# GpSimd adds the squares of six RMS norms; TensorE multiplies the mean matrix with one or two tiles a norm, behind the second weight slot

## The chip, the cores and the metric

One core of one Trainium2 chip runs the whole program. The metric is the device time of one execution in microseconds (us), the median of a few runs. Lower is better.

## What is computed

One inference step of a decoder trunk of two layers for 264 tokens (256 of a prompt and 8 samples of one token), in float32, with a model width of 1024:

```python
def rmsnorm(x, w):
    xf = x.astype(jnp.float32)
    y = xf * lax.rsqrt(jnp.mean(xf * xf, axis=-1, keepdims=True) + EPS)
    return (y * w.astype(jnp.float32)).astype(x.dtype)

def swiglu(h, wg, wu, wd):
    return (jax.nn.silu(h @ wg) * (h @ wu)) @ wd

for li in range(2):
    x = x + 0.5 * swiglu(rmsnorm(x, norm_ffn1[li]), ...)        # 1024 -> 2816 -> 1024
    h = rmsnorm(x, norm_mix[li])
    y = even_mixer(h, ...) if li == 0 else pool_mixer(h, ...)   # HGRN2 || gated DeltaNet; pooling
    x = x + y
    x = x + 0.5 * swiglu(rmsnorm(x, norm_ffn2[li]), ...)
y = rmsnorm(x, final_norm)
```

That makes seven RMS norms, numbered 0 to 6 in the kernel. The recurrent states are outputs too; the change does not touch them.

## The kernel before

**Layout.** Everything is held transposed: `x` has 8 tiles of 128 channels (partitions) by 264 tokens. The mean of squares over the 1024 channels is then a sum over partitions and tiles. TensorE makes it: ScalarE squares each tile of `x` into `hn`, and TensorE multiplies a 128x128 matrix `mean_w`, filled with 1/1024, with the eight tiles of `hn`, all summed in one PSUM bank (`sum_bank(n)`: bank 0, for norm 5 bank 2). Every row of that bank then holds the mean for each token.

**Weights.** All big matmuls use weights in pieces of 128x1024 floats, the slots, counted through the program by `s`. SyncE loads a slot into `raw` (4 buffers). ScalarE rounds it to `w_hi` (the ScalarE `tick`, L504 to L512) and VectorE makes `w_lo = raw - w_hi` (the VectorE `tick`, L1007 to L1014), each 3 slots ahead of TensorE. Activations are split in the same way, and `three` (L1500) makes each product from three matmuls. A slot is 24 of them in the stages that read `xw` or `x`, and 24 in the down projection. The semaphore `used` tells ScalarE that a slot is free, `lo_done` tells TensorE that one is ready.

**The norm is deferred.** The first product behind a norm does not wait for it: it takes `xw_hi`/`xw_lo`, the split of x times the norm's weight, and the factor `rstd` is multiplied in when the result leaves PSUM. `rstd` is made by a square root on ScalarE (`root`, L532, which waits for `ss_done` from TensorE) and a reciprocal on VectorE (`root_inverse`, L1042).

**An FFN** (`ffn`, TensorE L1544 to L1601) has 11 blocks of four slots: two slots give the gate in two PSUM banks, two give the up product in the next two. Then 22 slots of the down projection fill all eight banks. VectorE multiplies the gate by `rstd` (`gate`, L1065), ScalarE makes the SiLU (`silu`, L548), VectorE makes `factor` and `prod`. TensorE starts a block only when the SiLU of the block before is done (`silu_done`, L1552).

**The end of an FFN and the norm behind it** are the place of the change. For each of the eight tiles, in this order: VectorE adds the result to `x` (`residual`, L1021), ScalarE squares the tile (`square`, L514, semaphore `sq_done`) and writes `xw_hi` (L529), VectorE writes `xw_lo` (`weighted`, L1034). TensorE in its own order, with `norm` at L1526 and `first_slot` at L1539: the last down projections; four mean matmuls (tiles 0 to 3); the first weight slot of the next stage, which waits tile by tile for `xw_lo`; four more mean matmuls (tiles 4 to 7, the last raises `ss_done`); the second slot, and on. Norm 2 follows the even mixer's output projection, norm 5 the pooling mixer, and norm 6, the last, stands among the transposes that bring the result back (L1634 to L1649).

**After a norm, by stage.** The even mixer (norm 1) reads `xw` in its first four slots only, waits for the root behind two of them (L1180), and takes the really normed `hn`, split into `x_hi` and `x_lo` by `normed` (L536 and L1047), for the other 28. The pooling mixer (norm 4) keeps VectorE busy with window sums; ScalarE's `norm(5)` stands behind its copy of the last pooled rows (L489). The order on each engine is the order of the code. GpSimd (L1652 on) makes constants at the start and then only issues DMAs.

Of the kernel before, what the change touches and what calls it, by code (L numbers as in the profile page):

```python
# [29 lines left out]
ALU = mybir.AluOpType  # L30
# [25 lines left out]
SSB = 0  # L56
# [15 lines left out]
def build(nc, A, O_):  # L72
# [9 lines left out]
    with ctx:  # L82
# [68 lines left out]
        def SV(j):  # L151
# [4 lines left out]
            if j in (4, 5):  # L156
# [38 lines left out]
         par_in, x_in, x_T, dve_chain, act_chain, pool_chain) = [sem(n) for n in (  # L195
# [3 lines left out]
             "x_in", "x_T", "dve_chain",  # L199
# [21 lines left out]

        def sum_bank(n):

            return 2 if n == 5 else SSB

# [269 lines left out]
        def _(act):  # L495
# [502 lines left out]
        def _(dve):  # L998
# [22 lines left out]
            def residual(scale, ended, n=None, tiles=range(KD)):  # L1021

                for z in tiles:
                    d = ORDER5[z] if n == 5 else z
# [9 lines left out]
            def weighted(n, z):  # L1034

                dve.wait_ge(xwhi_done, 8 * n + z + 1)
                d = ORDER5[z] if n == 5 else z
# [24 lines left out]
            def ffn(n):  # L1062
                s0, b0 = S_FFN[n], NB * n

                def gate(b, i=None):  # L1065
# [4 lines left out]
                    st4 = 4 * ((b - b0 + 1) % 2)  # L1070
# [8 lines left out]
                def prod(b, i=None):  # L1079
                    dve.wait_ge(sg_done, v(b + 1, i, 2))  # L1080
                    dve.wait_ge(used, v(s0 + 4 * (b - b0) + 4, i, 8))
                    st4 = 4 * ((b - b0 + 1) % 2) + 2
# [41 lines left out]
                residual(0.5, lambda d: (res_done, 8 * n + d + 1), FFN_NORM[n] + 1)  # L1124
# [50 lines left out]
        def even_tensor(pe, mm, three, blk_slot, first_slot, xw_slot, norm):  # L1175
            tr = nc.tensor.transpose
            nwait = (lambda k: (xlo_done, k + 1))
            first_slot(S_PROJ, 2, 1)
            xw_slot(S_PROJ + 1, 1, 2, 1)
# [273 lines left out]
            norm(2)  # L1453

        def odd_tensor(pe, mm, three, first_slot, xw_slot, norm):
# [4 lines left out]
            first_slot(S_PIN, 2, 4)  # L1460
# [7 lines left out]
            for q in range(1, 8):  # L1468
                banks = (2 * (q // 2) + 2) % 8
                if banks == SSB and q % 2 == 0:  # L1470
# [4 lines left out]
                xw_slot(S_PIN + q, q % 2, banks, 4 if q == 1 else None)  # L1475
# [17 lines left out]
            norm(5)  # L1493
# [3 lines left out]
        def _(pe):  # L1497
# [28 lines left out]
            def norm(n, tiles=range(4), frees_slot=False):  # L1526

                for z in tiles:  # L1530
                    d = ORDER5[z] if n == 5 else z
                    pe.wait_ge(sq_done, 8 * n + z + 1)
                    ins = mm(ps[:, sum_bank(n), 0:TOK], mean_w[:, :], hn[:, d, :], start=z == 0, stop=z == KD - 1)  # L1533
                    if z == 0 and frees_slot:
                        ins.then_inc(used, 1)
                    if z == KD - 1:
                        ins.then_inc(ss_done, 1)

            def first_slot(s, banks, n):  # L1539
                pe.wait_ge(x_done, 8 * n + (4 if n == 5 else banks + 2))  # L1540
                xw_slot(s, 0, banks, n)
                norm(n, range(4, KD))

            def ffn(n):  # L1544
                s0, b0, nn = S_FFN[n], NB * n, FFN_NORM[n]

                def blk(b, i=None):
                    s = s0 + 4 * (b - b0)
                    banks = 4 * ((b - b0 + 1) % 2)
                    for q in range(4):  # L1550
                        if b and q == 0:
                            pe.wait_ge(silu_done, v(b, i, 2))  # L1552
                        if b and q == 2:
                            pe.wait_ge(prod_done, v(b, i, 2))
                        if b == b0 and q == 0:
                            first_slot(s, banks, nn)
                        else:
                            if b == b0 and q == 2:
                                pe.wait_ge(x_done, 8 * nn + 8)
                            xw_slot(s + q, q % 2, banks + 2 * (q // 2),  # L1560
                                    nn if b == b0 and (q == 1 or nn == 5) else None, i)
# [19 lines left out]
                down(0, range(4))  # L1581
                down(1, range(4))
                pe.wait_ge(prod_done, b0 + NB)
                down(0, range(4, 8)).then_inc(used, 1)
                down(1, range(4, 8)).then_inc(used, 1)
# [10 lines left out]
                for d in range(KD):  # L1596
# [3 lines left out]
                    down(KF - 1, [d]).then_inc(res_done, 1)  # L1600
                norm(nn + 1, frees_slot=True)  # L1601
# [189 lines left out]
```

## Time and profile before

| what | us |
|---|---|
| median of 3 runs | 1108.94 |
| lowest and highest | 1107.06, 1110.87 |
| span of the profiled execution, first to last instruction | 1105.1 |
| TensorE matmuls busy | 1077.1 (97%) |
| VectorE busy | 670.5 (61%) |
| ScalarE busy | 520.6 (47%) |
| GpSimd busy | 47.7 (4%) |
| mean granted TensorE clock, share of full speed | 0.993 |

The profile gives for the profiled execution its span alone; its device time with what lies before the first and after the last instruction is not told apart from the runs. The span is 2.0 us under the fastest run and 3.8 us under the median. Times in the rows are in us from the start of the span, durations of single instructions in ns where it says so. PE is TensorE, DVE is VectorE, ACT is ScalarE, POOL is GpSimd. `L1533` is a line of the kernel.

### The profile page before, as it was taken

Reading aid. Unit: us, or ns where it says so; the run is one execution under the profiler, and the core shown is the slowest. Engines: PE = TensorE matmul, PEld = TensorE weight load, DVE = VectorE, ACT = ScalarE, POOL = GpSimd, SP = SyncE. Lnnn points to the kernel's source line nnn. Section 1 sums busy time; section 2 is a strip of 40 time slices with the busy share of each in tenths; the row PEclk is TensorE's granted clock in tenths of the full one; section 3 lists DMA queues with packets and bytes.
Section 4 is the critical chain, followed back from the end, with each engine's and each line's share of the span. In section 5 each row is a group of like instructions: output and inputs, shape, how many; then the busy total and the mean of one; then the engine's idle time right before and its main releaser. Section 6 shows DMA issues by size and latency. Waiting matters only on the chain.

```text
span 1105.1 us, 21620 instructions
## 1 busy us (share of the span) xinstructions
PE 1077.1 (97%) x8541; PEld 1053.1 (95%) x8541; DVE 670.5 (61%) x872; ACT 520.6 (47%) x703; POOL 47.7 (4%) x118
## 2 busy tenths in 40 slices
PE   6999999999899998999999999999999999999998
PEld 5999999989799996999999999999999989999997
DVE  5766654587555655766665457666644876666542
ACT  5444443566574443554444346444433554444434
POOL 8100000010000110000000000000000000000000
PEclk9999999999899999999999999999999999999999
DMA  6666555878485521676565555665555446665551
GB/s 195 192 176 184 174 185 174 153 202 150 109 108 137 144 77 39 188 195 186 173 186 173 181 164 172 175 186 173 171 189 183 123 117 182 180 173 188 175 169 40
DMA packets 135061, 177.91 MB, mean 161 GB/s; under 512 B 5806, under 2 KB 120574, under 8 KB 134992
## 3 DMA queue, kind: packets, MB, share of 16 engines
q1 hardware_dynamic: 131616, 165.78, 52.9%
q0 software_dynamic: 3328, 11.38, 3.6%
q8 instruction: 37, 0.61, 0.2%
q14 instruction: 16, 0.13, 0.0%
q10 hardware_dynamic: 64, 0.02, 0.0%
HBM read 171.19 MB, written 6.52 MB: 161 GB/s over the span
## 4 chain that ended last, share of the span: by engine, by line
PE 91%; DVE 4%; ACT 2%; DMA 2%; issue 1%; ACTq 0%; SPq 0%; DVEq 0%
PE ps L1504 26%; PE ps L1505 26%; PE ps L1506 26%; PE ps L1533 2%; PE ps L1330 1%; DMA raw<-in_w_in_even 1%; PE ps L1337 1%; PE ps L1319 1%; ACT w_hi L512 1%; PE ps L1491 1%; DVE w_lo L1013 1%; PE ps L1300 1%; PE ps L1349 1%; PE ps L1609 1%; DVE C L632 0%
## 5 line engine op out<-in xcount | busy, mean ns | idle before, releaser
L1013 DVE TENSOR_TENSOR w_lo<-raw,w_hi 128x1024 fp32r<-128x1024 f32 x312 | 381.2, 1225 | 308.2 <-ACT w_hi L512 306.4
L512 ACT CAST w_hi<-raw 128x1024 fp32r<-128x1024 f32 x312 | 326.3, 1049 | 465.1 <-PE ps L1506 449.0
L1504 PE MATMUL ps<-xw_hi,w_hi 128*128 128x264 f32 x1504 | 431.1, 287 | 0.0
L1505 PE MATMUL ps<-xw_lo,w_hi 128*128 128x264 f32 x1504 | 429.9, 286 | 0.0
L1506 PE MATMUL ps<-xw_hi,w_lo 128*128 128x264 f32 x1504 | 429.1, 285 | 0.0
L1504 PEld LDWEIGHTS ps<-xw_hi,w_hi 128*128 128x128 f32 x1504 | 285.0, 190 | 0.7 <-issue 0.4
L1506 PEld LDWEIGHTS ps<-xw_hi,w_lo 128*128 128x128 f32 x1504 | 284.1, 189 | 0.0
L1505 PEld LDWEIGHTS ps<-xw_lo,w_hi 128*128 128x128 f32 x1504 | 283.8, 189 | 0.3
L1506 PE MATMUL ps<-a_hi,w_lo 128*128 (+1 forms) x704 | 200.6, 285 | 0.0
L1505 PE MATMUL ps<-a_lo,w_hi 128*128 (+1 forms) x704 | 200.3, 284 | 0.0
L1504 PE MATMUL ps<-a_hi,w_hi 128*128 (+1 forms) x704 | 200.3, 284 | 0.0
L1505 PEld LDWEIGHTS ps<-a_lo,w_hi 128*128 128x128 f32 x704 | 132.9, 189 | 0.0
L1506 PEld LDWEIGHTS ps<-a_hi,w_lo 128*128 128x128 f32 x704 | 132.7, 188 | 0.0
L1504 PEld LDWEIGHTS ps<-a_hi,w_hi 128*128 128x128 f32 x704 | 132.6, 188 | 0.0
L1504 PE MATMUL ps<-x_hi,w_hi 128*128 128x264 f32 x288 | 85.5, 297 | 4.0 <-DVE x_lo L923 1.9
L1505 PE MATMUL ps<-x_lo,w_hi 128*128 128x264 f32 x288 | 83.8, 291 | 0.0
L1506 PE MATMUL ps<-x_hi,w_lo 128*128 128x264 f32 x288 | 83.5, 290 | 0.0
L1504 PEld LDWEIGHTS ps<-x_hi,w_hi 128*128 128x128 f32 x288 | 56.1, 195 | 6.9 <-issue 4.0
L1505 PEld LDWEIGHTS ps<-x_lo,w_hi 128*128 128x128 f32 x288 | 56.0, 195 | 0.0
L1506 PEld LDWEIGHTS ps<-x_hi,w_lo 128*128 128x128 f32 x288 | 56.0, 194 | 0.0
L1083 DVE TENSOR_TENSOR pr<-sg,ps 128x528 f32<-128x528 f32 x44 | 31.0, 705 | 27.3 <-PE ps L1506 27.3
L1071 DVE TENSOR_TENSOR pr<-ps,rstd 128x528 f32<-128x528 f32 x44 | 31.1, 708 | 5.1 <-DVE a_lo L1089 1.4
(332 smaller groups left out, 823.5 us busy)
## 6 DMA issues: line engine op xcount, KB each, us to landing
raw<-in_ffn_w_gate SPq DMA_DIRECT2D x88, 512.0 KB, 3.7
raw<-in_ffn_w_up SPq DMA_DIRECT2D x88, 512.0 KB, 3.7
raw<-in_ffn_w_down SPq DMA_DIRECT2D x88, 512.0 KB, 3.4
raw<-in_w_in_even SPq DMA_DIRECT2D x32, 512.0 KB, 7.1
raw<-in_w_out_even SPq DMA_DIRECT2D x8, 512.0 KB, 4.1
raw<-in_pool_w_in SPq DMA_DIRECT2D x8, 512.0 KB, 3.4
out<-SBUFS POOLq DMA_DIRECT2D x4, 512.0 KB, 3.9
PT<-in_x_prompt SPq DMA_DIRECT2D x2, 512.0 KB
```

The lines of the kernel that those rows point to most:

```text
L512: nc.scalar.copy(w_hi[:, w % SPL, :], raw[:, w % RAW, :]).then_inc(hi_done, 1)
L1013: nc.vector.tensor_tensor(w_lo[:, w % SPL, :], raw[:, w % RAW, :], w_hi[:, w % SPL, :].bitcast(F32), ALU.subtract).then_inc(lo_done, 1)
L1071: nc.vector.tensor_tensor(pr[:, :, :], ps[:, st4:st4 + 2, 0:TOK], rstd2, ALU.mult)\
L1083: nc.vector.tensor_tensor(pr[:, :, :], sg[:, :, :], ps[:, st4:st4 + 2, 0:TOK], ALU.mult)\
L1300: ins = mm(ps[:, 7, 32 + 16 * h + 2 * b:34 + 16 * h + 2 * b], SV(h)[:, b, :], C[:, h:h + 5:4, PROMPT + b], start=True, stop=True)
L1319: ins = mm(psA[:, i, :], AT[:, i, :], T[:, i, :], start=True, stop=True)
L1330: ins = mm(psC[:, i, :], KS[:, i * P:(i + 1) * P], QP[:, i * P:(i + 1) * P], start=True, stop=True)
L1337: ins = mm(psA[:, i, :], l[:, i, :], m[:, i, :], start=True, stop=True)
L1504: mm(out, wh, hi, start=first, stop=False)
L1505: mm(out, wh, lo, start=False, stop=False)
L1506: return mm(out, wl, hi, start=False, stop=last)
L1533: ins = mm(ps[:, sum_bank(n), 0:TOK], mean_w[:, :], hn[:, d, :], start=z == 0, stop=z == KD - 1)
```

## The change

GpSimd gets `sum_squares(n)` for norms 1 to 6: it adds the squared tiles in place into the tile squared first, each add waiting for the square and for the add before it. It takes 8 tiles of norms 2, 3 and 5 and 7 of norms 1, 4 and 6. TensorE's `norm(n)` multiplies `mean_w` with that sum, and before it, where GpSimd took 7, with the eighth tile by itself. It stands behind the second weight slot instead of before the first and the second. Norm 0 keeps its eight mean matmuls. The sums go to other PSUM banks (`SUMB`), the block parity of three FFNs is turned for it, and the semaphore counts follow. In GpSimd's queue the loads of the pooling weights and of the pooling state (L1753 to L1759) come behind the sums of norm 3.

```diff
-SSB = 0
+SUMB = (7, 5, 7, 7, 0, 2, 0)
+POOLED = (0, 7, 8, 8, 7, 8, 7)
...
-            def norm(n, tiles=range(4), frees_slot=False):
...
-                for z in tiles:
-                    d = ORDER5[z] if n == 5 else z
-                    pe.wait_ge(sq_done, 8 * n + z + 1)
-                    ins = mm(ps[:, sum_bank(n), 0:TOK], mean_w[:, :], hn[:, d, :], start=z == 0, stop=z == KD - 1)
...
-            def first_slot(s, banks, n):
+            def norm(n):
+
+                alone = POOLED[n] < KD
+                if alone:
+                    pe.wait_ge(sq_done, 8 * n + KD)
+                    mm(ps[:, sum_bank(n), 0:TOK], mean_w[:, :], hn[:, KD - 1, :], start=True, stop=False)
+                pe.wait_ge(pooled, n)
+                mm(ps[:, sum_bank(n), 0:TOK], mean_w[:, :], hn[:, tile_of(n, 0), :], start=not alone, stop=True)\
+                    .then_inc(ss_done, 1)
+
+            def first_slots(s, banks, n):
                 pe.wait_ge(x_done, 8 * n + (4 if n == 5 else banks + 2))
                 xw_slot(s, 0, banks, n)
-                norm(n, range(4, KD))
+                if n == 0:
+                    norm_first(range(4, KD))
+                xw_slot(s + 1, 1, banks, n)
+                if n:
+                    norm(n)
...
-                    down(KF - 1, [d]).then_inc(res_done, 1)
-                norm(nn + 1, frees_slot=True)
+                    down(KF - 1, [d]).then_inc(res_done if d < KD - 1 else used, 1)
...
             for c in range(2):
                 back(c, 0)
-            norm(6, range(4, KD))
+            norm(6)
             back(2, 0)
...
+            def sum_squares(n):
+
+                acc = hn[:, tile_of(n, 0), :]
+                pool.wait_ge(sq_done, 8 * n + 1)
+                for z in range(1, POOLED[n]):
+                    pool.wait_ge(sq_done, 8 * n + z + 1)
+                    ins = G.tensor_tensor(acc, acc, hn[:, tile_of(n, z), :], ALU.add)
+                    if z < POOLED[n] - 1:
+                        link(ins)
+                ins.then_inc(pooled, 1)
...
-            pool.wait_ge(x_done, 8 * 3)
+            sum_squares(2)
+            sum_squares(3)
             for half in range(2):
                 pool.dma_start(group_w(half), pool_grp[0, 2 * half:2 * half + 2]
```

## Rows read from the trace of the kernel before

**Rows 1.** Groups of instructions, whole span: count, then busy us, mean ns, idle before

```profile
L1533 PE MATMUL ps<-hn,mean_w 128*128 128x264 f32 x112 | 29.1, 406 | 0.9 <-ACT hn L516 0.9
```

**Rows 2.** Timeline of TensorE at norms 3 and 2: start, length, instruction, count

```profile
660.20 1.94 PE L1533 MATMUL ps<-hn,mean_w 128*128 128x264 f32 x8
...
664.89 1.94 PE L1533 MATMUL ps<-hn,mean_w 128*128 128x264 f32 x8
...
462.93 0.61 PE L1533 MATMUL ps<-hn,mean_w 128*128 128x264 f32 x2
```

**Rows 3.** Timeline of ScalarE at norm 3, in brackets the idle time before

```profile
657.25 0.43 ACT L516 ACTIVATE hn<-x 128x264 f32<-128x264 f32 x1 [1.63 <-DVE x L1027]
...
665.93 1.28 ACT L534 ACT_TABLE_LOAD   x1
667.23 0.48 ACT L534 ACTIVATE rstd<-ps,eps 128x264 f32<-128x264 f32 x1
...
672.39 0.65 ACT L552 ACTIVATE sg<-pr 128x528 f32<-128x528 f32 x1 [0.26 <-DVE pr L1071]
```

**Rows 4.** Timeline of VectorE at norm 3

```profile
661.00 0.43 DVE L1027 SCALAR_TENSOR_TENSOR x<-ps,x 128x264 f32<-128x264 f32 x1
...
662.74 0.43 DVE L1027 SCALAR_TENSOR_TENSOR x<-ps,x 128x264 f32<-128x264 f32 x1
```

**Rows 5.** Groups of GpSimd, instructions that read SBUF, by shape

```profile
L1700 POOL TENSOR_SCALAR_AFFINE_SELECT SEL<-SEL 128x8 f32<-128x8 f32 x4 | 0.8, 192 | 0.1
L1676 POOL TENSOR_SCALAR_AFFINE_SELECT upper<-upper 128x128 f32<-128x128 f32 x1 | 0.3, 287 | 0.1
```

**Rows 6.** Timeline at the start, one GpSimd operation beside VectorE's and without it

```profile
15.41 3.57 DVE L1013 TENSOR_TENSOR w_lo<-raw,w_hi 128x1024 fp32r<-128x1024 f32 x3 [0.90 <-ACT par L596]
15.70 1.14 POOL L1690 TENSOR_SCALAR_AFFINE_SELECT lvl<-lvl 128x64 bf16<-128x64 bf16 x1
...
25.57 0.24 POOL L1690 TENSOR_SCALAR_AFFINE_SELECT lvl<-lvl 128x64 bf16<-128x64 bf16 x1
```

**Rows 7.** Timeline of TensorE at norm 1, the first product with the normed x

```profile
231.44 0.36 PE L1504 MATMUL ps<-x_hi,w_hi 128*128 128x264 f32 x1
```

**Rows 8.** Timeline of ScalarE at norm 2

```profile
469.65 0.48 ACT L534 ACTIVATE rstd<-ps,eps 128x264 f32<-128x264 f32 x1 [3.56 <-PE ps L1533]
...
474.93 0.65 ACT L552 ACTIVATE sg<-pr 128x528 f32<-128x528 f32 x1
```

**Rows 9.** Timelines from norm 4 to norm 5: VectorE, ScalarE

```profile
868.77 0.71 DVE L965 TENSOR_TENSOR PT<-ps,rstd 128x528 f32<-128x528 f32 x1 [0.36 <-PE ps L1506]
869.92 1.22 DVE L1013 TENSOR_TENSOR w_lo<-raw,w_hi 128x1024 fp32r<-128x1024 f32 x1 [0.45 <-ACT w_hi L512]
...
890.75 0.89 DVE L1027 SCALAR_TENSOR_TENSOR x<-ps,par,x 128x264 f32<-128x264 f32 x2
...
892.62 1.00 ACT L489 COPY C<-ps 23x1024 f32<-23x1024 f32 x1 [8.09 <-PE ps L1483]
```

**Rows 10.** Timelines at norm 5: TensorE, VectorE, ScalarE

```profile
895.56 0.39 PE L1533 MATMUL ps<-hn,mean_w 128*128 128x264 f32 x1
...
895.60 0.49 DVE L1027 SCALAR_TENSOR_TENSOR x<-ps,par,x 128x264 f32<-128x264 f32 x1
...
902.23 0.48 ACT L534 ACTIVATE rstd<-ps,eps 128x264 f32<-128x264 f32 x1 [0.75 <-PE ps L1533]
...
907.53 0.65 ACT L552 ACTIVATE sg<-pr 128x528 f32<-128x528 f32 x1
```

**Rows 11.** Timelines at norm 6: TensorE, ScalarE

```profile
1092.73 1.94 PE L1533 MATMUL ps<-hn,mean_w 128*128 128x264 f32 x8
1094.51 1.04 PE L1630 MATMUL ps<-ident,XH 128*128 128x128 f32 x8
...
1094.24 1.28 ACT L534 ACT_TABLE_LOAD   x1
1097.36 0.48 ACT L534 ACTIVATE rstd<-ps,eps 128x264 f32<-128x264 f32 x1 [1.84 <-PE ps L1533]
```

More of the change, by code:

```diff
@@ L194, in build @@
          gate_done, sg_done, p_ready, const_done,
-         par_in, x_in, x_T, dve_chain, act_chain, pool_chain) = [sem(n) for n in (
+         par_in, x_in, x_T, pooled, dve_chain, act_chain, pool_chain) = [sem(n) for n in (
              "hi_done", "lo_done", "used", "silu_done", "prod_done", "ahi_done",
@@ L1023, in residual @@
                 for z in tiles:
-                    d = ORDER5[z] if n == 5 else z
+                    d = tile_of(n, z)
                     dve.wait_ge(*ended(d))
@@ L1123, in ffn @@
                     tick(s1 + f)
-                residual(0.5, lambda d: (res_done, 8 * n + d + 1), FFN_NORM[n] + 1)
+                residual(0.5, lambda d: (res_done, 7 * n + d + 1) if d < KD - 1 else (used, s1 + KF), FFN_NORM[n] + 1)
                 tick(s1 + KF - 1)
@@ L1452, in even_tensor, with odd_tensor @@
                 ins.then_inc(used, 1)
-            norm(2)
-        def odd_tensor(pe, mm, three, first_slot, xw_slot, norm):
+        def odd_tensor(pe, mm, three, first_slots, xw_slot):
             tr = nc.tensor.transpose
@@ L1467, in odd_tensor @@
             ins.then_inc(st("pool_hist"), 1)
-            for q in range(1, 8):
+            for q in range(2, 8):
                 banks = (2 * (q // 2) + 2) % 8
-                if banks == SSB and q % 2 == 0:
+                if banks == sum_bank(4) and q % 2 == 0:
                     pe.wait_ge(root_done, 5)
@@ L1474, in odd_tensor @@
                     pe.wait_ge(x_done, 8 * 4 + banks + 2)
[L1475 removed]
+                xw_slot(S_PIN + q, q % 2, banks)
             pe.wait_ge(st("grp_in"), 32)
@@ L1548, in blk @@
                     s = s0 + 4 * (b - b0)
[L1549 to L1561, printed above, removed]
+                    banks = 4 * ((b - b0 + (n == 3)) % 2)
+                    if b:
+                        pe.wait_ge(silu_done, v(b, i, 2))
+                    if b == b0:
+                        first_slots(s, banks, nn)
+                    else:
+                        xw_slot(s, 0, banks, None, i)
+                        xw_slot(s + 1, 1, banks, None, i)
+                    if b:
+                        pe.wait_ge(prod_done, v(b, i, 2))
+                    if b == b0:
+                        pe.wait_ge(x_done, 8 * nn + 8)
+                    xw_slot(s + 2, 0, banks + 2, nn if b == b0 and nn == 5 else None, i)
+                    xw_slot(s + 3, 1, banks + 2, nn if b == b0 and nn == 5 else None, i)
                 blk(b0)
@@ L1580, in ffn @@
                 pe.wait_ge(alo_done, b0 + NB - 1)
-                down(0, range(4))
-                down(1, range(4))
+                free, last = (range(4), range(4, 8)) if n == 3 else (range(4, 8), range(4))
+                down(0, free)
+                down(1, free)
                 pe.wait_ge(prod_done, b0 + NB)
-                down(0, range(4, 8)).then_inc(used, 1)
-                down(1, range(4, 8)).then_inc(used, 1)
+                down(0, last).then_inc(used, 1)
+                down(1, last).then_inc(used, 1)
                 with pe.Fori(0, 2) as i:
@@ L1618, in _ @@
             pe.wait_ge(const_done, 1)
-            norm(0)
+            norm_first(range(4))
             ffn(0)
-            even_tensor(pe, mm, three, blk_slot, first_slot, xw_slot, norm)
+            even_tensor(pe, mm, three, blk_slot, first_slots, xw_slot)
             ffn(1)
             ffn(2)
-            odd_tensor(pe, mm, three, first_slot, xw_slot, norm)
+            odd_tensor(pe, mm, three, first_slots, xw_slot)
             ffn(3)
```

35 lines of the change are left out of this document (20 added, 15 removed).

## The prediction

> **What bounds the kernel now.** I read the page first: TensorE's matmuls cover 97% of a span of 1105.1 us, VectorE 61%, ScalarE 47%, and the chain that ended last is 91% TensorE. So a matmul taken away shortens the kernel, unless at its place TensorE then waits for something else. Second, the groups: the mean matmuls, L1533, are 112 records [rows 1]. A float32 product with `mean_w` is two records, so these are 56 products, 8 for each of seven norms. Third, the timeline at each norm. At the end eight records run from 1092.73 to 1094.51 [rows 11]: four products take 1.78 us, one takes 0.445. At norm 3 [rows 2] the last down projection ends at 660.20, four products follow, one weight slot, four products from 664.89, the second slot. A slot is 664.89 - 660.20 - 1.78 = 2.91 us. Nowhere there does TensorE pause, so the products of the norm are paid in full. Fourth, ScalarE and VectorE over the same stretch, since the norm's result has its own way: sum, square root, reciprocal, gate, SiLU, and TensorE may begin the second block of an FFN only behind that SiLU [rows 3].
>
> **What is removed.** 48 products in norms 1 to 6 become 9 (2, 1, 1, 2, 1, 2). 39 x 0.445 = 17.4 us of TensorE's time go. That is the ceiling; the rest of the work is to see how much of it turns into a wait, norm by norm.
>
> **What an add costs GpSimd.** The trace has no GpSimd operation with two inputs. The nearest read one: 192 ns for 8 elements in a partition and 287 ns for 128 [rows 5], thus 0.79 ns an element. Both operands of 264 elements one behind the other would be 192 + 512 x 0.79, about 600 ns. The low end is 0.3 us (as one operand of 128), the high end 1.6 us: 0.6 and a wait behind one long VectorE operation, which the next paragraph shows. I take 0.6, and 0.67 a step with its semaphore. By the Trainium skill (GPSIMD Engine Reference, "Performance versus the Vector engine"), such an add takes about 2.6 cycles an element at 1.2 GHz, which makes an estimate of some 0.6 us; no run here shows it yet, and the sum does not need it.
>
> **GpSimd and VectorE side by side.** One and the same selection of 128x64 takes 0.24 us with VectorE's `w_lo` absent and 1.14 beside it [rows 6]: it ends when VectorE's operation ends. VectorE hardly pays: three `w_lo` in 3.57 us, against 1.22 for one alone [rows 9]. But that selection reads 64 elements, an add 528, so VectorE may wait for an add. For two tiles VectorE now needs 1.74 us (661.00 to 662.74 [rows 4]), with two `xw_lo` in it, each about 0.49 as the like VectorE operation of [rows 10], and some idle time. If each add keeps the reads for 0.5 us, 2 x 0.49 + 2 x 0.5 = 1.98, which is 0.24 over, and over half of the tiles fall so: I take 0.4 us of delay of the whole ScalarE and VectorE chain at a norm where adds meet `xw_lo`. The low end is nothing; the high end, with the reads kept for 0.6 and a semaphore at each change of hands, is (2.18 - 1.74) x 3.5 pairs = 1.5 us. The Trainium skill (SBUF — State Buffer, "Who interferes with whom") says more than the row: whoever starts first holds the shared ports for its whole instruction and the other fully blocks. The row agrees for GpSimd behind VectorE and leaves the other way round open; that rule is the first rival.
>
> **Norm by norm.** *Norm 3.* New order on TensorE: slot 660.20 to 663.11, slot to 666.02, one product to 666.46, two slots to 672.28. Now the second block begins at 664.89 + 1.78 + 3 x 2.91 = 675.40. TensorE alone would win 7 x 0.445 = 3.12. But the SiLU ends at 672.39 + 0.65 = 673.04 [rows 3], and nothing on its way gets earlier: the root starts at 667.23 behind ScalarE's own table load, not behind TensorE's sum. The sum behind the second slot is ready at about 666.65, just in time. So TensorE stops for 0.8 us in front of the second block: 2.3 are left, and with the delay of 0.4, 1.9.
> *Norm 2.* Its squares come in groups between weight splits, so adds meet little. The root does wait for TensorE here (3.56 us idle before it [rows 8]). New: two slots from 462.93 [rows 2] to 468.75, product to 469.20, finished at about 469.4, root 0.25 earlier than 469.65, SiLU's end from 475.58 to 475.33; TensorE would be there at 475.02. Now the second block starts at 462.93 + 3.56 + 4 x 2.91 = 478.13. Gain 2.7.
> *Norm 1.* Slots 5 and on of the even mixer need the normed x. The root stands behind ScalarE's own table load as at norm 3, VectorE's reciprocal, eight normed tiles and a weight split follow, and TensorE starts its fifth slot, the first of these, at 231.44 [rows 7]. It gets to that point earlier and waits for the same chain. Gain nothing; the delay of 0.4 is a loss, since TensorE has no slack left before it.
> *Norm 4.* Six products less, 2.67. Behind it VectorE is busy to the residual at 890.75. Of its idle time 0.36 + 0.45 us (before L965 and before the next split [rows 9]) go with TensorE's earlier slots, and the delay takes 0.4 of that back. ScalarE's copy of the last rows now ends at 893.62 and would end at 890.95; the first residual tile is there at about 890.8. I take 2.6.
> *Norm 5,* against the same start 895.56 [rows 10]: the first slot waits for the fourth residual, 895.60 + 0.49, so it starts at 896.15, where four products hid this so far. Two slots to 901.97, product to 902.42, sum at 902.6 against a root at 902.23 now: root and SiLU 0.4 later, SiLU's end 908.6. Second block now 895.56 + 3.56 + 4 x 2.91 = 910.76. Gain 2.1, less the delay 1.7.
> *Norm 6.* No `xw_lo`, so no meeting. Last square ends at about 1093.8, the sum of seven is there too, two products to 1094.8. The root then waits for its table load alone, to 1095.52 [rows 11], against 1097.36. Gain 1.8.
> Sum: -0.4 + 2.7 + 1.9 + 2.6 + 1.7 + 1.8 = **10.3 us**.
>
> **Costed at nothing.** The moved loads of pooling weights and state: three DMAs of half a megabyte now start at norm 3 instead of 2, still far ahead of the pooling mixer that reads them; if they slowed the weight loads there, ScalarE would wait on a DMA. GpSimd's load of the conv history comes behind the sums of norm 1, and TensorE transposes it several slots later. The two stores of pooled rows stand just before the sums of norm 5 and delay the first; the adds catch up before the eighth square. The turned bank parity moves no instruction. The extra semaphore counts are sequencer time. If GpSimd's queue were late at a norm, TensorE would stand at `pooled` with all later slots behind it.
>
> **Rivals.**
> *Full blocking.* Every add holds VectorE for its whole length and more. For: the 1.14 us selection [rows 6]. Against: VectorE's three splits beside it ran at full pace, 1.19 each. Delay 1.5 instead of 0.4 at norms 1, 3, 5, and 0.6 lost at norm 4 where VectorE is full: -1.5 + 2.6 + 0.8 + 2.0 + 0.6 + 1.8 = 6.3 us, 1102.6. This is also what the Trainium skill's rule on the ports (same page and section) would tend to.
> *The adds are the new wait (slower).* Their chain starts with the second square, about 658.5 (the first starts at 657.25 [rows 3], one ScalarE tile is 0.75 and the square 0.43). With 1.6 us an add and 0.07 between, seven end at 670.2, and the root 3.6 later than now. Then norm 3 loses 1.3, norm 5 1.5, norm 1 1.9, norm 6 2.7 (six adds from 1089.4), norm 4 still gains 1.4 and norm 2 2.7: together 3.3 slower, 1112.2. It changes sign at an add of about 1.5 us. For: GpSimd's 1.14 in company. Against: VectorE is free between tiles, and 0.6 fits its alone rows.
> *No gain that shows.* The chain of ScalarE and VectorE is the bound at every norm as at norm 1, and TensorE just waits longer: only norm 6 and part of 2 are left, or the adds take 1.3 to 1.5. 0 to 3 us, about 1107.5. Against: ScalarE's table load is the only thing in front of the root at norm 3, and TensorE was behind the SiLU by 2.3 us.
> *More than forecast.* The chain reorders itself better than I see, no delay at all: 12 to 13 us, 1096.4.
>
> **How the numbers follow.** The sum is made in one profiled execution of span 1105.1, 3.8 us under the median of the runs; what lies around the span is taken as unchanged, so the difference is put on the median: 1108.9 - 10.3 = 1098.6. About 0.3% (3.3 us) is what a measurement can tell from no change. Chances: forecast (7 to 12 us of gain) 0.55, full blocking 0.20, no gain 0.11, the adds as wait 0.09, more 0.05. Faster by over 0.3%: the forecast, the last and full blocking, 0.80. Within 0.3%: 0.11. Slower: 0.09. The range: from the case of more, 1096.4, less 1 for the runs' own spread, 1095.5, up to the middle of full blocking and no gain, 1105.5.
>
> **What would show it.** L1533 with 34 records (17 products). At norm 3 TensorE's gap of about 0.8 to 1.2 us before the second block, released by the SiLU; GpSimd adds of 0.6 us (1 us and more where they wait), `xw_lo` at 0.5 to 0.6 in the mean; the second block at norm 3 about 13.3 us behind the last down projection, now 15.2. It would be wrong if TensorE stands at L1533 for `pooled`, if ScalarE waits for a weight DMA at norm 3, or if `w_lo` and `xw_lo` grow by more than half.

## The result, and the profile after

The changed kernel takes 1099.92 us (median of 4 runs, 1097.34 to 1102.12) against 1108.64 for the kernel before (1107.06 to 1110.87): a ratio of 0.9909, 95% interval 0.989 to 0.9929. That is 8.7 us faster, where 10.3 were forecast; the forecast of 1098.6 lies 1.3 us under the measured time.

The two profiled spans, 1105.1 and 1100.4 us, differ by 4.7 us only, so the first step is to cut both into stretches that begin and end at the start of a product. "Norm 3" is the time from the last down projection ahead of norm 3 to the first one behind it, and so on; "norm 1" ends where the mixer's first product with the normed x starts, "norm 4" ends at the last product of the pooling groups, and "norm 6" at the first product of the last stage that uses the root. The down projections between them take 64.24 us each in both kernels.

| stretch, us | before | after | gained | forecast |
|---|---|---|---|---|
| start to norm 1 | 216.01 | 215.04 | 0.97 | 0 |
| norm 1 | 15.42 | 16.19 | -0.77 | -0.4 |
| even mixer | 231.37 | 236.60 | -5.23 | 0 |
| norm 2 | 133.04 | 130.25 | 2.79 | 2.7 |
| norm 3 | 132.97 | 131.54 | 1.43 | 1.9 |
| norm 4 | 38.05 | 35.53 | 2.52 | 2.6 |
| norm 5 | 133.03 | 132.14 | 0.89 | 1.7 |
| norm 6 | 5.52 | 3.46 | 2.06 | 1.8 |
| the six norms | | | 8.9 | 10.3 |

The six norms give 8.9 us, about what the medians say. The loss of 5.2 us in the even mixer goes with the granted clock: over that stretch it was 0.97 in the mean before and 0.95 after. If TensorE bounds the whole stretch, the missing 3% of 231.4 and 5% of 236.6 are time lost, which makes an estimate of 4.9 us between them. The kernel before, profiled a second time, had 0.96 and took 233.95 there instead of 231.37. Apart from the first adds of norm 2 near its end, no instruction of the stretch differs. The windows view of a part of it shows the difference (columns: us, busy time and count of TensorE, its weight loads, VectorE, ScalarE, GpSimd, the granted clock, the DMA share, GB/s). Before, before again, after:

```profile
306.00:318.00 12.00, 12.00 (x94) 11.29 (x93) 5.60 (x5) 7.29 (x19) 0.00 (x0) 1.00 0.99 121
```
```profile
306.00:318.00 12.00, 12.00 (x81) 11.29 (x80) 5.38 (x5) 6.59 (x17) 0.00 (x0) 0.86 0.92 114
```
```profile
306.00:318.00 12.00, 12.00 (x64) 11.23 (x64) 4.94 (x5) 3.97 (x10) 0.00 (x0) 0.72 0.92 94
```

TensorE is busy throughout in all three, at 2.4 GHz in the first (1.00) and partly at 1.2 GHz in the others. It had been busy and at 1.00 from 290 to 306 in all three, so no wait right before it explains the difference, and why the grant varies from execution to execution stays open. The stretch took 236.93 in a kernel with the products of before and 231.18 in one with the sums of the change (the table below), so neither length belongs to one of the two; that the change has no part in how often the lower clock comes is not shown. The norms are therefore compared stretch by stretch, and whole kernels by their medians.

Now the page and the groups of after. The page:

```profile
span 1100.4 us, 21542 instructions
...
PE 1066.8 (97%) x8463; PEld 1042.2 (95%) x8463; DVE 676.0 (61%) x872; ACT 521.1 (47%) x703; POOL 79.1 (7%) x157
...
PE 85%; DVE 8%; ACT 3%; issue 2%; DMA 2%; ACTq 0%; SPq 0%; DVEq 0%
```

TensorE has 78 records fewer, which are the 39 products. Its share of the chain that ended last fell from 91% to 85%, and VectorE's rose from 4% to 8%: what the removed products leave behind is in part a wait for VectorE. The groups (busy us, mean ns, idle before):

```profile
L1733 POOL TENSOR_TENSOR hn<-hn 128x264 f32<-128x264 f32 x39 | 30.6, 785 | 773.8 <-ACT hn L521 772.8
...
L1532 PE MATMUL ps<-hn,mean_w 128*128 128x264 f32 x16 | 5.7, 518 | 0.9 <-ACT hn L521 0.9
L1541 PE MATMUL ps<-hn,mean_w 128*128 128x264 f32 x6 | 1.9, 402 | 0.0
L1543 PE MATMUL ps<-hn,mean_w 128*128 128x264 f32 x12 | 3.7, 394 | 0.0
...
L1043 DVE SCALAR_TENSOR_TENSOR xw_lo<-x,par,xw_hi 128x264 fp32r<-128x264 f32 x48 | 30.1, 648 | 3.3 <-ACT xw_hi L534 3.3
```

The 112 records of [rows 1] are now 16 + 6 + 12 = 34, as the change says. L1543, which waits for `pooled`, has no idle time in front: no matmul stands for GpSimd's sum. Only at norm 6 does the weight load of L1543 wait 0.4 us for it, and the root is behind its table load there all the same. An add takes 785 ns in the mean, and `xw_lo` went from a mean of 488 ns to 648.

Norm 3 in the timelines (start, length, instruction, idle before). VectorE:

```profile
662.76 0.42 DVE L1032 SCALAR_TENSOR_TENSOR x<-ps,x 128x264 f32<-128x264 f32 x1
663.11 0.71 DVE L1043 SCALAR_TENSOR_TENSOR xw_lo<-x,par,xw_hi 128x264 fp32r<-128x264 f32 x1
...
664.08 0.74 DVE L1043 SCALAR_TENSOR_TENSOR xw_lo<-x,par,xw_hi 128x264 fp32r<-128x264 f32 x1
664.75 0.42 DVE L1032 SCALAR_TENSOR_TENSOR x<-ps,x 128x264 f32<-128x264 f32 x1
...
671.66 1.22 DVE L1018 TENSOR_TENSOR w_lo<-raw,w_hi 128x1024 fp32r<-128x1024 f32 x1 [1.32 <-ACT w_hi L517]
672.80 1.79 DVE L1049 RECIPROCAL rstd<-rstd 128x264 f32<-128x264 f32 x1
674.63 0.71 DVE L1076 TENSOR_TENSOR pr<-ps,rstd 128x528 f32<-128x528 f32 x1
```

GpSimd beside it:

```profile
662.76 0.76 POOL L1733 TENSOR_TENSOR hn<-hn 128x264 f32<-128x264 f32 x1 [0.22 <-ACT hn L521]
663.78 0.75 POOL L1733 TENSOR_TENSOR hn<-hn 128x264 f32<-128x264 f32 x1 [0.26 <-ACT hn L521]
```

Each `xw_lo` starts 0.3 us behind an add, gets longer (0.71 to 0.74 us, 0.49 before), and ends 0.3 us behind the end of that add: 663.82 behind 663.52, 664.82 behind 664.53. The adds do not get longer. These seven take what the six at norm 6 take, where there is no `xw_lo` (count, then ns: least, median, most):

```profile
L1733 POOL TENSOR_TENSOR hn<-hn x6: 740/755/766, 1087.0 to 1091.1; 128x264 f32<-128x264 f32 x6
```
```profile
L1733 POOL TENSOR_TENSOR hn<-hn x7: 752/759/762, 660.8 to 666.7; 128x264 f32<-128x264 f32 x7
```

The same pair of tiles that took 1.74 us [rows 4] takes 664.75 - 662.76 = 1.99. The two `xw_lo` grow by some 0.24 us each; half of that falls into time in which VectorE had waited for `xw_hi` before:

```profile
661.59 0.49 DVE L1038 SCALAR_TENSOR_TENSOR xw_lo<-x,par,xw_hi 128x264 fp32r<-128x264 f32 x1 [0.15 <-ACT xw_hi L529]
```

ScalarE and TensorE:

```profile
670.21 0.48 ACT L539 ACTIVATE rstd<-ps,eps 128x264 f32<-128x264 f32 x1
...
675.37 0.64 ACT L557 ACTIVATE sg<-pr 128x528 f32<-128x528 f32 x1 [1.50 <-DVE pr L1076]
```
```profile
668.68 0.61 PE L1543 MATMUL ps<-hn,mean_w 128*128 128x264 f32 x2
669.35 0.36 PE L1506 MATMUL ps<-xw_hi,w_hi 128*128 128x264 f32 x1
...
676.15 0.38 PE L1506 MATMUL ps<-xw_hi,w_hi 128*128 128x264 f32 x1 [0.73 <-ACT sg L557]
```

TensorE, which nowhere paused at this norm [rows 2], now stops ahead of its second block and is released by the SiLU: the stop that the forecast named. ScalarE's timeline also shows a wait inside ScalarE's part of the way that was not named: the SiLU had come 0.26 us behind ScalarE's last work [rows 3], and now ScalarE stands 1.50 us for `pr`. VectorE took a weight split of 1.22 us in front of the reciprocal, although the root was ready at 670.21 + 0.48 = 670.69.

### The profile page after: what moved, and what is told of

It reads as the page before. It is cut to its first block, busy times and chain, and to the rows that moved or that the text cites. A ratio compares the mean times of both kernels' runs of the same rounds, so it can differ in the third digit from the quotient of the medians.

```text
span 1100.4 us, 21542 instructions
## 1 busy us (share of the span) xinstructions
PE 1066.8 (97%) x8463; PEld 1042.2 (95%) x8463; DVE 676.0 (61%) x872; ACT 521.1 (47%) x703; POOL 79.1 (7%) x157
## 4 chain that ended last, share of the span: by engine, by line
PE 85%; DVE 8%; ACT 3%; issue 2%; DMA 2%; ACTq 0%; SPq 0%; DVEq 0%
PE ps L1506 25%; PE ps L1507 25%; PE ps L1508 24%; ACT w_hi L517 2%; DVE xw_lo L1043 1%; PE ps L1334 1%; DVE w_lo L1018 1%; DMA raw<-in_w_in_even 1%; PE ps L1341 1%; DVE x L1032 1%; PE ps L1323 1%; DVE rstd L1049 1%; DVE PT L979 1%; PE ps L1304 1%; PE ps L1353 1%
## 5 line engine op out<-in xcount | busy, mean ns | idle before, releaser
L1018 DVE TENSOR_TENSOR w_lo<-raw,w_hi 128x1024 fp32r<-128x1024 f32 x312 | 380.9, 1224 | 302.6 <-ACT w_hi L517 300.8
L1733 POOL TENSOR_TENSOR hn<-hn 128x264 f32<-128x264 f32 x39 | 30.6, 785 | 773.8 <-ACT hn L521 772.8
L1507 PEld LDWEIGHTS ps<-x_lo,w_hi 128*128 128x128 f32 x288 | 58.3, 203 | 0.0
L1508 PEld LDWEIGHTS ps<-x_hi,w_lo 128*128 128x128 f32 x288 | 58.3, 202 | 0.0
```

The costliest lines, as they stand in the source:

```text
L1018: nc.vector.tensor_tensor(w_lo[:, w % SPL, :], raw[:, w % RAW, :], w_hi[:, w % SPL, :].bitcast(F32), ALU.subtract).then_inc(lo_done, 1)
L1507: mm(out, wh, lo, start=False, stop=False)
L1508: return mm(out, wl, hi, start=False, stop=last)
L1733: ins = G.tensor_tensor(acc, acc, hn[:, tile_of(n, z), :], ALU.add)
```

## The experiments

Two theories were to be told apart. By the first (Theory A in the expectations), the gain is what the removed products leave once TensorE runs into the ScalarE and VectorE chain, and the adds cost only what they take from VectorE. By the second, the adds (or GpSimd's order) set the time, or the gain comes from the new order of TensorE rather than from the products removed. The stretches of all runs, in us:

| kernel | norm 1 | 2 | 3 | 4 | 5 | 6 | mixer | median us | ratio to before |
|---|---|---|---|---|---|---|---|---|---|
| before | 15.42 | 133.04 | 132.97 | 38.05 | 133.03 | 5.52 | 231.37 | 1108.64 | |
| changed | 16.19 | 130.25 | 131.54 | 35.53 | 132.14 | 3.46 | 236.60 | 1099.92 | 0.9909 |
| no adds | 15.45 | 130.25 | 130.78 | 35.42 | 131.07 | 3.46 | 234.03 | 1097.05 | 0.9906 |
| before and adds | 15.82 | 133.05 | 133.05 | 38.07 | 133.07 | 5.53 | 236.93 | 1109.73 | 1.0014 |
| order only | 18.03 | 133.31 | 133.35 | 38.07 | 134.21 | 5.89 | 231.71 | 1111.65 | 1.0042 |
| reciprocal first | 16.19 | 129.83 | 130.60 | 35.59 | 131.72 | 3.46 | 236.45 | 1100.53 | 0.9925 |
| norm 1 by TensorE | 15.43 | 130.20 | 131.54 | 35.57 | 132.18 | 3.46 | 236.47 | 1098.27 | 0.9895 |
| before, recip. first | 15.43 | 133.04 | 132.98 | 38.05 | 133.03 | 5.52 | 234.94 | 1108.62 | 0.9995 |
| both | 15.42 | 129.83 | 130.53 | 35.57 | 131.73 | 3.46 | 233.95 | 1097.25 | 0.9892 |
| changed again | 16.19 | 130.25 | 131.53 | 35.58 | 132.13 | 3.46 | 236.45 | 1102.03 | 0.9934 |
| two adds a tile | 19.10 | 130.93 | 137.54 | 43.22 | 138.33 | 8.99 | 231.18 | 1130.62 | 1.0199 |
| before again | 15.44 | 133.04 | 132.97 | 38.05 | 133.03 | 5.52 | 233.95 | 1109.82 | 1.0009 |

### Without the adds

```diff
-                for z in range(1, POOLED[n]):
-                    pool.wait_ge(sq_done, 8 * n + z + 1)
-                    ins = G.tensor_tensor(acc, acc, hn[:, tile_of(n, z), :], ALU.add)
...
-                ins.then_inc(pooled, 1)
+                pool.wait_ge(sq_done, 8 * n + POOLED[n])
+                G.memset(mark[:, :], 0.0).then_inc(pooled, 1)
```

It leaves out the adds of the squares, so each mean lacks most of its tiles; TensorE's order and work are those of the change.

> The changed kernel without GpSimd's adds: a one-column memset behind the last square of a norm raises the semaphore, so TensorE sums two tiles at most and the norm's value is another. Stretches are taken in the profile of TensorE, from the last product before a norm to the first behind it that waits for it: norm 1 15.42 us before and 16.19 changed; norm 3 (last down product to the first of the next FFN's) 132.97 and 131.54; norm 5 133.03 and 132.14. Theory A (the adds and xw_lo block each other and delay ScalarE's and VectorE's chain): xw_lo falls from 648 to about 490 ns, norm 1 is back at 15.4, norm 3 falls to about 130.7, norm 5 to about 131.0, norms 2, 4 and 6 stay within 0.3; 2.5 to 3 us less than the changed kernel in all. Rival B (what is missing against the forecast is not contention but the sequence: the root is late by itself): norms 3 and 5 stay within 0.2 of the changed kernel.

Measured: norm 1 0.74 us shorter than in the changed kernel, norm 3 0.76, norm 5 1.07, norm 4 0.11, norms 2 and 6 the same: 2.7 us in all. Against before the norms gain 11.6 us, and the forecast's terms without its delay make 0 + 2.7 + 2.3 + 2.6 + 2.1 + 1.8 = 11.5. So the products' part was sized right, and the adds' price was not. Adds meet `xw_lo` at norms 1 to 5; norms 1, 3 and 5 pay for it, norm 4 hardly and norm 2 not at all. `xw_lo` is back at the length of before:

```profile
L1044 DVE SCALAR_TENSOR_TENSOR xw_lo<-x,par,xw_hi 128x264 fp32r<-128x264 f32 x48 | 22.6, 489 | 5.4 <-ACT xw_hi L535 5.1
```

The medians (1097.05 against 1099.92) agree in sign, but the intervals of their ratios overlap; the stretches carry this verdict.

Where norm 5 pays is in TensorE's timeline of the changed kernel and then of this one:

```profile
894.97 0.36 PE L1506 MATMUL ps<-xw_hi,w_hi 128*128 128x264 f32 x1 [0.96 <-issue]
...
901.52 0.60 PE L1543 MATMUL ps<-hn,mean_w 128*128 128x264 f32 x2
```
```profile
890.74 0.36 PE L1507 MATMUL ps<-xw_hi,w_hi 128*128 128x264 f32 x1 [0.47 <-issue]
...
896.67 0.61 PE L1544 MATMUL ps<-hn,mean_w 128*128 128x264 f32 x2
```

The first slot starts 0.96 - 0.47 = 0.49 us later, since the fourth residual, which it waits for, stands behind a longer `xw_lo`, and the two slots take 901.52 - 894.97 = 6.55 us instead of 5.93, since TensorE runs into tiles that are not there yet. Together 1.11 us, the price of the adds at this norm. At norm 3 the same two slots take 668.68 - 662.44 = 6.24 us.

### The adds alone, in the kernel before

```diff
+            def sum_squares(n, tiles):
+
+                pool.wait_ge(sq_done, 8 * n + 1)
+                for z in range(1, tiles):
+                    pool.wait_ge(sq_done, 8 * n + z + 1)
+                    link(G.tensor_tensor(own[:, :], own[:, :], own[:, :], ALU.add))
```

The calls stand where the change has them, and nobody reads `own`.

> The kernel before, and GpSimd makes as many adds of the same shape at the same squares, on a tile of its own that nobody reads. Theory A: xw_lo rises from 488 to about 650 ns and VectorE's pair of tiles from 1.74 to 1.99 us, but TensorE still has products and slots in front of the SiLU at norms 2, 3, 4, 5, so only norm 1 pays, 0.8 us: 15.4 to 16.2; total 1109.4. Rival C (adds cost where they stand, whatever TensorE does): 0.8 at norms 1, 3, 5 each, about 2.5 us in all, 1111.

```profile
L1721 POOL TENSOR_TENSOR own<-own 128x264 f32<-128x264 f32 x39 | 26.8, 688 | 780.1 <-ACT hn L517 778.8
...
L1039 DVE SCALAR_TENSOR_TENSOR xw_lo<-x,par,xw_hi 128x264 fp32r<-128x264 f32 x48 | 26.0, 562 | 6.1 <-ACT xw_hi L530 5.6
```

Norm 1 loses 0.40 us (0.8 expected), the others 0 to 0.08, as expected: with eight products on TensorE, ScalarE and VectorE have slack everywhere but at norm 1. The ratio, 0.9999 to 1.0029, can't be told from none. Outside norm 1 the price of the adds thus exists only once the products are gone. It is not quite the same add: one that reads one tile twice takes 0.62 us with VectorE idle (norm 6), the add of the change, two tiles of `hn`, 0.74 to 0.77. At norm 1 an `xw_lo` beside it takes 0.61 to 0.62 us, beside the add of the change 0.73, against 0.49 alone: it grows by half as much, and norm 1 paid half.

At norm 5 of this kernel VectorE mostly starts first. There the `xw_lo` keeps its length and the add is the longer one, 0.91 us instead of 0.62:

```profile
902.17 0.49 DVE L1039 SCALAR_TENSOR_TENSOR xw_lo<-x,par,xw_hi 128x264 fp32r<-128x264 f32 x1
```
```profile
902.24 0.91 POOL L1721 TENSOR_TENSOR own<-own 128x264 f32<-128x264 f32 x1
```

### The order alone

```diff
             def norm(n):
-                alone = POOLED[n] < KD
...
+                pe.wait_ge(sq_done, 8 * n + KD)
+                for z in range(KD):
+                    ins = mm(ps[:, sum_bank(n), 0:TOK], mean_w[:, :], hn[:, tile_of(n, z), :], start=z == 0, stop=z == KD - 1)
+                ins.then_inc(ss_done, 1)
```

GpSimd adds nothing; all eight products stand behind the second slot.

> The changed order and banks, but all eight products of a norm on TensorE, behind the second slot, and no adds. Theory A says that the order alone loses, since the sum is then finished 2.5 to 3.5 us later than before and the SiLU or the reciprocal behind it ends last: norm 1 17.8 (15.42 before), norm 2 133.3 (133.04), norm 3 133.3 (132.97), norm 4 39 (38.05), norm 5 134.0 (133.03), norm 6 5.8 (5.52): 5 us slower than before, about 1114. Rival D (TensorE's time alone counts): as before, 1108.6.

Measured: 1111.65 us, ratio 1.0042 (1.0023 to 1.006): slower than before. Norm 1 loses 2.61 us, norm 5 1.18, norms 2, 3 and 6 between 0.27 and 0.38. ScalarE at norm 3 tells why:

```profile
672.56 0.48 ACT L539 ACTIVATE rstd<-ps,eps 128x264 f32<-128x264 f32 x1 [2.61 <-PE ps L1540]
...
677.73 0.64 ACT L557 ACTIVATE sg<-pr 128x528 f32<-128x528 f32 x1 [1.50 <-DVE pr L1076]
```

The root now waits 2.61 us for the sum. A place behind the second slot is good only for a short sum. The expected loss of 1 us at norm 4 did not come (38.07 against 38.05); what hides it stays open.

### VectorE's order: the reciprocal ahead of a weight split

```diff
                     tick(s, i)
-                    tick(s + 1, i)
                     if b > b0:
+                        tick(s + 1, i)
                         lo_a(b - 1, i)
                     else:
                         root_inverse(FFN_NORM[n])
                     gate(b, i)
+                    if b == b0:
+                        tick(s + 1, i)
                     tick(s + 2, i)
```

> The changed kernel with one order turned on VectorE: in the first block of an FFN the reciprocal and the gate come before the split of the fourth slot ahead. Theory A says that the wait of 1.0 us in front of the second block at norm 3, of 0.3 to 0.4 at norms 2 and 5, is this chain (split 1.2, reciprocal 1.8, gate 0.7, SiLU): norm 3 falls from 131.54 to about 130.6, norm 2 from 130.25 to 130.0, norm 5 from 132.14 to 131.8; 1.5 us less in all, about 1098.4. Rival E (the wait goes over to the split of the fourth slot, which the second block reads too): norm 3 stays within 0.2 of 131.54.

```profile
670.75 1.80 DVE L1049 RECIPROCAL rstd<-rstd 128x264 f32<-128x264 f32 x1 [0.39 <-ACT rstd L539]
672.59 0.71 DVE L1076 TENSOR_TENSOR pr<-ps,rstd 128x528 f32<-128x528 f32 x1
673.21 2.35 DVE L1018 TENSOR_TENSOR w_lo<-raw,w_hi 128x1024 fp32r<-128x1024 f32 x2
```

The reciprocal starts at 670.75 instead of 672.80, and norms 2, 3 and 5 gain 0.42, 0.94 and 0.42 us (0.25, 0.9 and 0.3 expected). So at these norms TensorE waits for the SiLU's chain and not for GpSimd. The whole kernel does not show it: its median is 1100.53 (ratio 0.9925, 0.9903 to 0.9947), where about 1098.4 was expected, and that of the changed kernel was 1099.92. The stretches alone carry this verdict. The same edit in the kernel before:

> The kernel before with the same turned order on VectorE as in the changed kernel's variant (reciprocal and gate before the split of the fourth slot, first block of an FFN). Theory A: before, TensorE comes to the second block 2.3 us behind the SiLU, so an earlier SiLU gives nothing: norms 2, 3, 5 stay at 133.04, 132.97, 133.03 within 0.1, time as before, 1108.6. Rival G (the order is worth 0.4 to 0.9 a norm by itself): 132.6, 132.0, 132.6.

All six norms within 0.01 us of before, ratio 0.9995 (0.9981 to 1.001). In the kernel before TensorE hid this order; the change uncovers it.

### Norm 1 by TensorE, as before

```diff
-SUMB = (7, 5, 7, 7, 0, 2, 0)
+SUMB = (7, 0, 7, 7, 0, 2, 0)
...
-                if n == 0:
-                    norm_first(range(4, KD))
+                if n < 2:
+                    norm_first(range(4, KD), n)
                 xw_slot(s + 1, 1, banks, n)
-                if n:
+                if n > 1:
...
-            sum_squares(1)
```

The first four products of norm 1 stand behind its last down projection again.

> The changed kernel with norm 1 left to TensorE as before: four products behind the down projection, four behind the first slot, no adds, sum in bank 0. Theory A: TensorE has room there and only the adds cost something, so norm 1 goes from 16.19 back to 15.4 and the other norms stay (130.25, 131.54, 35.53, 132.14, 3.46, within 0.2); 0.8 us less, about 1099.1. Rival F (norm 1 profits from the saved products after all): norm 1 above 16.2.

Norm 1 is back at 15.43 us (0.76 less than in the changed kernel), the others within 0.05. The median, 1098.27 (ratio 0.9895, 0.9875 to 0.9915), has the right sign, but by its interval it can't be told from that of the changed kernel. In the changed kernel the mixer's first product with the normed x is released late; the line of before is [rows 7]:

```profile
223.48 0.39 PE L1506 MATMUL ps<-xw_hi,w_hi 128*128 128x264 f32 x1 [1.27 <-ACT rstd L539]
...
231.23 0.36 PE L1506 MATMUL ps<-x_hi,w_hi 128*128 128x264 f32 x1 [1.64 <-issue]
```

The six products taken from TensorE there, 2.67 us, come back as these two waits, 2.91 us, and the adds' delay comes on top.

### Both edits

> The changed kernel with norm 1 on TensorE and the reciprocal and gate first. If the two are independent, as Theory A has it: norm 1 15.4, norm 2 129.83, norm 3 130.60, norm 4 35.6, norm 5 131.7, norm 6 3.46, that is 2.6 us less than the changed kernel by stretches; about 1097.2.

1097.25 us, ratio 0.9892 (0.9873 to 0.9911), the lowest ratio of all. Each norm stands within 0.07 us of where one of the two edits alone put it, so they are independent. By the stretches it gains 11.5 us at the norms against 8.9; the interval of its ratio still overlaps that of the changed kernel's first measurement, but not that of the changed kernel measured beside it (0.9918 to 0.9949, below). Of the 4.8 us between those two medians the norms explain 2.6.

### Two adds a tile

```diff
                     pool.wait_ge(sq_done, 8 * n + z + 1)
+                    link(G.tensor_tensor(own[:, :], own[:, :], own[:, :], ALU.add))
                     ins = G.tensor_tensor(acc, acc, hn[:, tile_of(n, z), :], ALU.add)
```

> The changed kernel, and in front of each of GpSimd's adds one more of the same shape on a tile of its own, so that a step takes about 1.6 us instead of 0.76 to 1.0. It puts the slower rival of the prediction (adds of 1.6 us a step, 3.3 us slower than before) to the test. Expected by the chain of adds: the sum of seven at norm 3 ends near 11.3 us behind the second square, 4.5 later than in the changed kernel, and TensorE stands at the wait for the sum: norm 3 134.2 (131.54 changed, 132.97 before), norm 5 135.5, norm 1 17.3, norm 4 37, norm 6 8.3, norm 2 130.5; 13 us slower than the changed kernel, about 1113, which is 4 to 5 us slower than before. Rival H (GpSimd's adds are hidden however long, since the sum is wanted late): norms 3 and 5 within 0.5 of the changed kernel.

Measured: 1130.62 us, ratio 1.0199 (1.0164 to 1.0233), 17.6 us over what was expected. TensorE and GpSimd at norm 3:

```profile
672.60 1.25 PE L1544 MATMUL ps<-hn,mean_w 128*128 128x264 f32 x2 [5.41 <-POOL hn L1735]
673.27 0.80 PE L1507 MATMUL ps<-xw_hi,w_hi 128*128 128x264 f32 x1
```
```profile
666.34 1.49 POOL L1734 TENSOR_TENSOR own<-own 128x264 f32<-128x264 f32 x1
...
667.90 1.60 POOL L1735 TENSOR_TENSOR hn<-hn 128x264 f32<-128x264 f32 x1
669.58 0.62 POOL L1734 TENSOR_TENSOR own<-own 128x264 f32<-128x264 f32 x1
670.29 0.74 POOL L1735 TENSOR_TENSOR hn<-hn 128x264 f32<-128x264 f32 x1
```

Two sizes were missed. Two adds fall beside VectorE's weight splits and take 1.49 and 1.60 us instead of the 0.62 and 0.74 of the two behind them, so this one tile of the seven costs 3.24 us. The sum of norm 3 ends at 672.55, 13.0 us behind its start, where some 11.3 were expected, and TensorE stands 5.41 us for `pooled`. And the clock falls, as the windows view shows (same columns as above):

```profile
661.00:670.00 9.00, 6.19 (x51) 5.97 (x50) 6.98 (x12) 7.12 (x13) 8.29 (x10) 1.00 0.16 45
670.00:672.60 2.60, 0.00 (x1) 0.00 (x1) 0.00 (x0) 0.00 (x0) 2.36 (x5) 0.55 0.88 260
672.60:676.00 3.40, 3.40 (x13) 3.19 (x14) 0.67 (x1) 2.11 (x3) 1.95 (x3) 0.50 0.60 167
676.00:679.00 3.00, 3.00 (x23) 3.00 (x22) 2.97 (x4) 1.53 (x2) 0.00 (x0) 0.82 1.06 310
```

The fall comes while TensorE still stands, idle since 667.19. Behind the wait it runs at 0.50, that is 1.2 GHz, and comes back to 2.4 GHz only between 676 and 679. This is the slower rival's mechanism, made real: GpSimd's chain as the wait, with all of TensorE behind it.

### Each kernel once more, unaltered

> The changed kernel once more, unaltered, beside the others on one chip: stretches of the norms as in its first profile within 0.1 (16.19, 130.25, 131.54, 35.53, 132.14, 3.46), while the even mixer's stretch (236.6 then, 231.4 in the profile of before) moves by several us with the granted clock and not with the change.

> The kernel before once more, unaltered: the norms' stretches as in its first profile within 0.1 (15.42, 133.04, 132.97, 38.05, 133.03, 5.52). The even mixer's stretch, 231.4 us there and 234 to 237 in most other profiles, is expected to come out longer than 231.4 with a lower granted clock in it, since nothing in the changed kernel touches it.

Changed: 1102.03 us, ratio 0.9934 (0.9918 to 0.9949); before: 1109.82, ratio 1.0009 (0.9986 to 1.0033). Each norm comes back within 0.05 us, while the mixer moves by 2.6 us between the two profiles of the kernel before. So stretches separate a few tenths, and medians of whole kernels move by about 2 us from one set of runs to another. Two sets of the same changed kernel gave 0.9909 and 0.9934: 8.7 and 6.6 us faster than the kernel before beside it. The second interval leaves out the 10.3 us of the forecast, the first holds it, and the norms give 8.9 both times.

## Why the prediction was right, and where it was off

The account below goes by the stretches of the norms. That the whole kernel came within 1.3 us of the forecast is in part luck: the second set of runs lay 2.1 us higher.

**The ceiling and the products removed:** right. 34 records of the mean are left, 39 products of 0.445 us went, and without the adds the norms gain 11.6 us where the terms without a delay make 11.5.

**The price of an add:** 0.6 us taken, 0.785 measured in the mean, and 0.74 to 0.77 where VectorE does not hold it up. The 0.6 fits an add that reads one tile twice, 0.62. By the Trainium skill (GPSIMD Engine Reference, "Performance versus the Vector engine") the estimate was 0.6 us as well; the trace agrees for that add only, and the add of the change, with two different tiles, takes 0.14 us more even when alone. No matmul waited for it.

**GpSimd and VectorE side by side:** this is the term that was mis-sized. That VectorE would wait for an add was right. The pair of tiles took 1.99 us against the 1.98 worked out, and that agreement is partly luck: no row shows an add that keeps the reads for 0.5 us; an add runs 0.75 us, has 0.41 of them left when `xw_lo` starts, and lengthens it by 0.24. The step that failed is the last one, "over half of the tiles fall so: I take 0.4 us of delay": with 0.25 us a pair it should be 3.5 x 0.25 = 0.9 where all tiles fall so, and the runs show 0.74, 0.76 and 1.07 us at norms 1, 3 and 5. At norms 3 and 5 seven of the eight `xw_lo` meet an add, at norms 1 and 4 six: at norm 3 an add starts with the residual of a later tile, some 0.3 us ahead of an `xw_lo`, and is still under way. Norm 4 paid 0.11 us. In sum 2.7 us instead of the 1.2 that the forecast carried (0.4 at norms 1, 3 and 5; the 0.4 of norm 4 was covered by idle time). These 1.5 us, less 0.1 by which the products brought more than forecast, are the 1.4 us by which the norms fell short. The sign "`xw_lo` at 0.5 to 0.6 in the mean" failed with it, at 0.648.

**Full blocking** is what the rows show, at a lower price than this rival gave it. By the Trainium skill (SBUF — State Buffer, "Who interferes with whom"), a VectorE instruction with two inputs in SBUF contends with a GpSimd instruction that reads SBUF, and the order of issue decides who blocks. The trace agrees: in the changed kernel all 30 `xw_lo` that start while an add runs, 0.05 to 0.48 us behind its start, end 0.29 to 0.30 us behind its end, whatever their length (0.56 to 0.99 us); the one add that starts during a weight split, 0.18 us behind it, ends 0.62 us behind the split's end and takes 1.66 us. The Trainium skill calls the shared ports an exclusive lock there, and speaks of a full block in so many words for VectorE's two-port modes. These rows show one for two inputs in SBUF. Whoever starts second waits for the first and gives back only some 0.1 to 0.2 us of its own length. The rival's 1.5 us a norm did not come, because VectorE does not wait for a whole add: it waits for what is left of one, and half of that falls into idle time.

**Norm 3:** the stop ahead of the second block came, released by the SiLU. The second block starts 676.15 - 662.44 = 13.7 us behind the start of the norm, where 13.3 was forecast and 15.2 stood before; the 0.4 over the forecast is the part of the delay that the forecast left out (0.76 against 0.4). Not seen was that the split in front of the reciprocal is on this way: another order is worth 0.94 us here and nothing in the kernel before.

**Norm 1:** nothing gained and the delay lost, as worked out, with -0.77 for -0.4. **Norm 2:** 2.79 for 2.7 (the forecast's own times, 478.13 - 475.33, make 2.8). The forecast took it that adds meet little here, and that was wrong: four `xw_lo` take 0.66 to 0.99 us, and an add beside a split 1.66. It costs nothing (130.25 with the adds and without), because the adds are done at 471.03 and the root waits for TensorE's product with the sum, which starts at 473.78. **Norm 4:** 2.52 for 2.6. **Norm 6:** 2.06 for 1.8; the root waited for its table load alone, as forecast.

**Norm 5:** 0.89 for 1.7, the largest miss. Without adds 1.96 of the 2.1 are there. The adds then take 1.07: the first slot, which without the four products in front has nothing to hide behind, starts 0.49 us later than without them, and the two slots take 0.62 us more, since their tiles come slower than TensorE takes them. Without the adds the slot starts 0.85 us behind the start of the last group product, where the forecast has it too (896.15 - 895.34 = 0.81); with them 1.34.

**Costed at nothing:** no such item shows at any norm without adds, which together differ from the forecast by 0.1 us; none of the items was tried by itself. The start to norm 1 was 0.97 us shorter; over all profiles of this case it lies between 214.78 and 216.01, whichever of the edits is in, and its cause was not tried.

**The slower rival** did not come: an add took 0.785 us. Where its sign changes, put at an add of 1.5 us, was not tried: with two adds a tile the steps at norm 3 took 1.5 to 3.2 us, 1.86 in the mean. The kernel was then 2% slower, not the 0.3% that the rival gave for 1.6 us a step, because the steps beside weight splits were longer and because the clock fell during the long wait, which the rival did not price.

**The upper end of the range** was to be the middle of 1102.6 and 1107.5, which is 1105.05 and not 1105.5.

## What to carry to other kernels

Work taken from the engine that bounds is worth what it was only until that engine meets the next chain, so list, place by place, the slack of every other engine first; six places here ranged from -0.8 to 2.8 us for nearly equal cuts. When a helper engine is started by the same event that starts another engine's work on the same tiles, expect nearly every one of them to collide, and price them all: who starts second waits for what is left of the first. And read again the order on the engine that became the new bound: an exchange of two VectorE instructions was worth nothing before this change and 1.8 us at three norms after it.

## What the runs showed of the hardware

A GpSimd add and a VectorE operation with two inputs in SBUF do not share the time: whoever starts second waits. An `xw_lo` of 0.49 us that starts during an add takes 0.56 to 0.99 us and ends 0.29 to 0.30 us behind the add, while the add keeps its 0.75. Turned round, an add of 0.62 us that starts 0.07 us behind an `xw_lo` takes 0.91, and that `xw_lo` keeps 0.49. It holds for the weight split of 1024 elements too, in both directions. The kernel with two adds a tile has a split that starts first and keeps the add, 1.49 us instead of 0.62, and then one that starts during this add and takes 1.65 us instead of 1.22:

```profile
667.26 1.65 DVE L1019 TENSOR_TENSOR w_lo<-raw,w_hi 128x1024 fp32r<-128x1024 f32 x1
```

In the changed kernel only one add meets a split, and the split is first, so its splits keep their mean, 1224 ns against 1225. VectorE's residual, which has one of its two large inputs in PSUM, keeps its 0.42 us beside the adds.

A wait of 5.4 us on TensorE cost more than its length: the granted clock fell to 0.50 during it and stayed there for the 3.4 us behind it, while the wait of 0.73 us at the same place in the changed kernel left it at 1.00:

```profile
661.00:681.00 20.00, 19.20 (x151) 18.34 (x150) 16.66 (x23) 14.94 (x24) 7.08 (x10) 1.00 0.69 201
```
